# Hybrid attention and expert layer: the last expert's rows are added to the output on their own

## What is computed

```python
aff = jax.nn.softmax(jnp.einsum('bnd,de->bne', h, w_router).astype(jnp.float32), axis=-1)
gates, idx = lax.top_k(aff.swapaxes(1, 2), cap)            # cap = 128 tokens an expert
xe = h[bidx, idx]
hid = jax.nn.silu(jnp.einsum('becd,edf->becf', xe, w_gate)) * jnp.einsum('becd,edf->becf', xe, w_up)
ye = jnp.einsum('becf,efd->becd', hid, w_down) * gates[..., None].astype(h.dtype)
x = x + g2 * jnp.zeros_like(h).at[bidx, idx].add(ye)
return rms_norm(x, final_norm_g)
```

## Time and profile before

| | us |
|---|---|
| median of 3 runs | 2086.47 |
| lowest, highest | 2085.27, 2088.32 |
| the profiled execution's own time | 2086.9 |
| its span (first to last instruction) | 2085.1 |
| TensorE busy | 1858.8 (89%) |
| DVE busy | 1606.0 (77%) |
| ACT busy | 1303.9 (63%) |
| POOL busy | 270.8 (13%) |

### The profile page before, as it was taken

How to read it: one execution, slowest core, us unless ns; L and a number is a source line. 1 busy time by engine, 2 the same in 40 slices (tenths; PEclk the granted TensorE clock), 3 DMA queues, 4 the chain that set the end, 5 groups by cost and what they waited for, 6 DMA issues and landing times.

```text
span 2085.1 us, 28008 instructions
## 1 busy us (share of the span) xinstructions
PE 1858.8 (89%) x8691; PEld 1459.7 (70%) x8691; DVE 1606.0 (77%) x2065; ACT 1303.9 (63%) x1919; POOL 270.8 (13%) x291
## 2 busy tenths in 40 slices
PE   6799578998899899826999999999999999999993
PEld 3677456666666666515888888888888888888882
DVE  5577627668676766557999988889899989998983
ACT  3554127657566666524777777777777777777772
POOL 0233203101111110100111000110011001100011
PEclk8999779999999999957999999999999999999997
DMA  8356354101201110026999999999999999999985
GB/s 344 101 172 182 91 173 116 44 29 51 60 19 42 60 43 28 21 111 266 412 390 385 373 401 383 387 376 380 401 388 376 371 402 391 377 376 400 372 323 201
DMA packets 103794, 511.75 MB, mean 245 GB/s; under 512 B 12048, under 2 KB 36024, under 8 KB 53056
## 3 DMA queue, kind: packets, MB, share of 16 engines
q1 hardware_dynamic: 95824, 484.65, 61.4%
q0 software_dynamic: 4608, 16.78, 3.2%
q10 hardware_dynamic: 3312, 9.70, 1.3%
HBM read 481.19 MB, written 27.28 MB: 244 GB/s over the span
## 4 chain that ended last, share of the span: by engine, by line
PE 51%; issue 2%; DVE 2%; DMA 1%; ACT 0%; POOL 0%; ACTq 0%; POOLq 0%; SPq 0%
PE banks L1513 33%; PE banks L1538 16%; PE banks L1525 1%; PE banks L1494 1%; DVE topi L1384 1%; DVE top L1382 1%; DVE cand L1385 1%; DMA xe<-h_scratch,icol 0%; DMA acc_scratch<-ysc,idx_s 0%; DVE raw L1477 0%; ACT raw L1371 0%; DMA raw<-acc_scratch 0%; POOL fst L1298 0%; POOL fst L1300 0%; POOL gate_s L1281 0%
## 5 line engine op out<-in xcount | busy, mean ns | idle before, releaser
L1416 DVE TENSOR_TENSOR w_lo<-raw,w_hi 128x2048 fp32r<-128x2048 f32 x256 | 574.6, 2285 | 67.4 <-ACT w_hi L1320 67.4
L1320 ACT ACTIVATE w_hi<-raw 128x2048 fp32r<-128x2048 f32 x256 | 470.2, 1916 | 8.3 <-DMA raw<-in_w_exp 8.2
L1513 PE MATMUL banks<-w_hi,x_hi 128*128 128x512 f32 x1024 | 405.5, 396 | 1.4 <-DVE x_lo L1410 1.4
L1513 PE MATMUL banks<-w_hi,x_lo 128*128 128x512 f32 x1024 | 399.9, 390 | 0.0
L1513 PE MATMUL banks<-w_lo,x_hi 128*128 128x512 f32 x1024 | 399.4, 390 | 0.0
L1424 DVE TENSOR_TENSOR d_lo<-raw,d_hi 128x1024 fp32r<-128x1024 f32 x256 | 296.1, 1216 | 1.5 <-ACT d_hi L1342 1.4
L1342 ACT ACTIVATE d_hi<-raw 128x1024 fp32r<-128x1024 f32 x256 | 258.0, 1060 | 40.1 <-DMA raw<-in_w_exp 26.7
L1513 PEld LDWEIGHTS banks<-w_hi,x_lo 128*128 128x128 f32 x1024 | 192.7, 188 | 40.8
L1513 PEld LDWEIGHTS banks<-w_hi,x_hi 128*128 128x128 f32 x1024 | 192.9, 188 | 39.7 <-DVE x_lo L1410 1.8
L1513 PEld LDWEIGHTS banks<-w_lo,x_hi 128*128 128x128 f32 x1024 | 193.1, 189 | 38.1
L1014 DVE TENSOR_TENSOR ptl<-banks,pth 128x384 fp32r<-128x384 f32 x320 | 176.3, 554 | 56.0 <-ACT pth L960 51.7
(11 more groups left out here) (202 smaller groups left out, 2756.8 us busy)
## 6 DMA issues: line engine op xcount, KB each, us to landing
raw<-in_w_exp SPq DMA_DIRECT2D x384, 1024.0 KB, 7.8
a_ring<-in_w_mod SPq DMA_DIRECT2D x32, 512.0 KB, 4.7
qt<-q_scratch SPq DMA_DIRECT2D x64, 192.0 KB, 3.5
a_slot<-in_w_mod SPq DMA_DIRECT2D x8, 1024.0 KB, 12.3
a_w_raw<-in_w_in SPq DMA_DIRECT2D x3, 2048.0 KB, 30.8
q_scratch<-a_qst SPq DMA_DIRECT2D x16, 384.0 KB, 3.8
a_xt<-in_x ACTq DMA_DIRECT2D x8, 512.0 KB, 3.3
xr<-in_x SPq DMA_DIRECT2D x8, 512.0 KB, 4.1
```

The lines of the kernel that those rows point to most:

```text
L1320: act.activation(w_hi[which][c][:, :], raw[which][c][:, :], ACT.Copy).then_inc(s["hi_done"], 1)
L1416: dve.tensor_tensor(w_lo[which][c][:, :], raw[which][c][:, :], w_hi[which][c][:, :].bitcast(F32), ALU.subtract).then_inc(s["lo_done"], 1)
L1513: i = pe.matmul(psum[:, 2 * (j % 2) + which, :], x_[par][:, k, :], w_, start=(k == 0 and w_ is hi and x_ is x_hi), stop=(k == KD - 1 and x ...
```

## The change

The eight loads of `acc_scratch` no longer wait for the last expert: SP waits for 15 scatters and for the raw buffers, loads all eight tiles, and later issues the eight stores itself, each when its tile is normalised. POOL, once scatter 14 has landed, gathers the 128 rows of `acc_scratch` that expert 15 chose into `xe`. DVE normalises tiles 0 to 3, then makes the result of expert 15, adds `xe` to it (`ysc`), normalises tiles 4 to 7 and then `ysc` as a ninth set of rows. ACT's nine squares write their unused squares to two PSUM banks instead of a raw buffer, and `ysc` is the ninth. When the eight stores have landed, POOL writes `ysc` over the 128 rows of `out` with an indirect DMA (no addition), and the program's last wait is for that. Rows that expert 15 chose are so normalised twice, once without it, and the second version replaces the first.

The diff, without the hunks that only pass `out_rows` on:

```diff
@@ before.py +++ after.py @@
+    out_rows = out.rearrange("b n d -> (b n) d")
...
@@ -1187,18 +1188,18 @@
     h_hi, h_lo = (sb(f"h_{n}", [P, NK, P], F32R, M) for n in ("hi", "lo"))
     d_hi, d_lo = ([sb(f"d_{n}{k}", [P, D], F32R, M) for k in range(NK)] for n in ("hi", "lo"))
     ysc = sb("ysc", [P, D], F32, M)
+    sqj = psum[:, 0:2, :].rearrange("p a n -> p (a n)")
     carry = sb("carry", [P, 2], F32, M)
     fgain = sb("fgain", [P, D], F32, M)
 
     xa = [raw[t // 4][t // 2 % 2][:, t % 2 * D:(t % 2 + 1) * D] for t in range(TL)]
-    sqj = raw[2][0][:, 0:D]
-    fst = sb("fst", [P, TL, 3], F32, M)
+    LAST = TL
+    fst = sb("fst", [P, TL + 1, 3], F32, M)
     s = {n: sem("m_" + n) for n in (
         "top_order", "cand_zero", "cand_done", "merged", "carried", "top_done", "top_t", "cols_done", "idx_g", "x_in", "x_mm", "x_a", "x_b",
         "gate_mm", "up_mm", "sil_done", "hid_done", "ht_mm", "ht_done", "down_mm", "y_done", "y_out", "sel_done",
-        "hi_done", "lo_done", "d_hi_done", "d_lo_done", "h_lo_done", "fg_in", "a_done", "mean", "rstd", "norm_done")}
+        "hi_done", "lo_done", "d_hi_done", "d_lo_done", "h_lo_done", "fg_in", "a_done", "mean", "rstd", "norm_done", "last_sum", "last_out")}
     raw_in = [[sem(f"raw_in{w}{c}") for c in range(2)] for w in range(3)]
-    NX = TL
     xa_in = unit_in
     xa_out = sem("xa_out")
     Y, HB, XB = 4, 6, 7
@@ -1243,9 +1244,14 @@
             load(E - 1, NJ - 1, 2, 0)
             load(E - 1, NJ - 1, 2, 1)
 
-            sp.wait_ge(s["y_out"], 16 * E)
+            sp.wait_ge(s["y_out"], 16 * (E - 1))
             for t in range(TL):
+                if t % 2 == 0:
+                    sp.wait_ge(s["lo_done"], 4 * (NJ * E - 1) + t // 2 + 1)
                 sp.dma_start(xa[t][:, :], acc_d.rearrange("(t p) d -> t p d", p=P)[t]).then_inc(xa_in[t], 16)
+            for t in range(TL):
+                sp.wait_ge(s["norm_done"], t + 1)
+                sp.dma_start(out_d[t], xa[t][:, :]).then_inc(xa_out, 16)
 
         @block.gpsimd
         def _(pool):
@@ -1292,12 +1298,26 @@
                 gather(e + 2)
                 scatter(e)
             scatter(E - 2)
-            scatter(E - 1)
-            for t in range(TL):
+
+            pool.wait_ge(s["y_out"], 16 * (E - 1))
+            pool.tensor_copy(idx_s[:, :], icol[:, E - 1:E])
+            pool.tensor_copy(gate_s[:, :], gcol[:, E - 1:E]).then_inc(s["sel_done"], 1)
+            pool.wait_ge(s["sel_done"], E)
+            pool.wait_ge(s["x_mm"], 2 * E)
+            carrier(2 * E - 2)
+            pool.indirect_dma_start(out=xe[:, :], out_offset=None, in_=acc_d,
+                                    in_offset=bass.IndirectOffsetOnAxis(ap=idx_s[:, 0:1], axis=0)).then_inc(s["x_in"], 16)
+            for t in range(TL + 1):
                 pool.wait_ge(s["a_done"], t + 1)
                 pool.tensor_tensor(fst[:, t, 1:2], fst[:, t, 0:1], eps_c[:, 1:2], ALU.add).then_inc(s["mean"], 1)
                 pool.wait_ge(s["mean"], t + 1)
                 pool.tensor_tensor(fst[:, t, 2:3], fst[:, t, 1:2], eps_c[:, 0:1], ALU.pow).then_inc(s["rstd"], 1)
+            pool.wait_ge(xa_out, 16 * TL)
+            pool.wait_ge(s["norm_done"], TL + 1)
+            carrier(2 * E - 1)
+            pool.indirect_dma_start(out=out_rows, out_offset=bass.IndirectOffsetOnAxis(ap=idx_s[:, 0:1], axis=0),
+                                    in_=ysc[:, :], in_offset=None).then_inc(s["last_out"], 16)
+            pool.wait_ge(s["last_out"], 16)
 
         @block.scalar
         def _(act):
@@ -1362,17 +1382,13 @@
             split_down(E - 1, NJ - 1)
             turn(E - 1, NJ - 1)
 
-            def store(t):
-                act.wait_ge(s["norm_done"], t + 1)
-                act.dma_start(out_d[t], xa[t][:, :]).then_inc(xa_out, 16)
             for t in range(TL):
                 act.wait_ge(xa_in[t], 16 * 2)
                 after(act, s["a_done"], t)
-                act.activation(sqj[:, :], xa[t][:, :], ACT.Square, accum_out=fst[:, t, 0:1]).then_inc(s["a_done"], 1)
-                if t >= 1:
-                    store(t - 1)
-            store(TL - 1)
-            act.wait_ge(xa_out, 16 * NX)
+                act.activation(sqj, xa[t][:, :], ACT.Square, accum_out=fst[:, t, 0:1]).then_inc(s["a_done"], 1)
+            act.wait_ge(s["last_sum"], 1)
+            act.wait_ge(s["a_done"], TL)
+            act.activation(sqj, ysc[:, :], ACT.Square, accum_out=fst[:, LAST, 0:1]).then_inc(s["a_done"], 1)
 
         @block.vector
         def _(dve):
@@ -1467,15 +1483,27 @@
                     x_part(0, 0, 0)
                     x_part(0, 0, 1)
             every(expert, dve)
+            FIRST = 4
             dve.wait_ge(s["fg_in"], 16)
-            dve.tensor_scalar(fgain[:, :], fgain[:, :], ROOT, None, ALU.mult)
+            dve.tensor_scalar(fgain[:, :], fgain[:, :], ROOT, None, ALU.mult).then_inc(s["fg_in"], 16)
             split_down(E - 1, NJ - 1)
             turn(E - 1, NJ - 1)
+
+            def final(t, rows_):
+                dve.wait_ge(s["rstd"], t + 1)
+                if t == 0:
+                    dve.wait_ge(s["fg_in"], 32)
+                dve.scalar_tensor_tensor(out=rows_, in0=rows_, scalar=fst[:, t, 2:3], in1=fgain[:, :],
+                                         op0=ALU.mult, op1=ALU.mult).then_inc(s["norm_done"], 1)
+            for t in range(FIRST):
+                final(t, xa[t][:, :])
             result(E - 1)
-            for t in range(TL):
-                dve.wait_ge(s["rstd"], t + 1)
-                dve.scalar_tensor_tensor(out=xa[t][:, :], in0=xa[t][:, :], scalar=fst[:, t, 2:3], in1=fgain[:, :],
-                                         op0=ALU.mult, op1=ALU.mult).then_inc(s["norm_done"], 1)
+            dve.wait_ge(s["y_done"], E)
+            dve.wait_ge(s["x_in"], 16 * (E + 1))
+            dve.tensor_tensor(ysc[:, :], ysc[:, :], xe[:, :], ALU.add).then_inc(s["last_sum"], 1)
+            for t in range(FIRST, TL):
+                final(t, xa[t][:, :])
+            final(LAST, ysc[:, :])
 
         @block.tensor
         def _(pe):
```

More of the change, by code:

```diff
@@ L132, in build @@
         K.close()
-        nc_phase_m(nc, ctx, sem, sb, a, psum, ident, rows, aff, eps_c, h2_d, acc_d, out_d, unit_in)
+        nc_phase_m(nc, ctx, sem, sb, a, psum, ident, rows, aff, eps_c, h2_d, acc_d, out_d, out_rows, unit_in)
 def after(eng, sem_, v):
@@ L1151, in nc_phase_b, with nc_phase_m @@
     B.close()
-def nc_phase_m(nc, ctx, sem, sb, a, psum, ident, rows, aff, eps_c, h2_d, acc_d, out_d, unit_in):
+def nc_phase_m(nc, ctx, sem, sb, a, psum, ident, rows, aff, eps_c, h2_d, acc_d, out_d, out_rows, unit_in):
     G1, SH2, SC2, G2 = range(4)
```

## The result

The median of four runs is 2072.52 us (2069.51 to 2073.81), against 2086.94 for four runs of the kernel before. These two medians lie 14.4 apart. The ratio on record, which is not the quotient of the two medians, is 0.9923 with a 95% interval of 0.9909 to 0.9937, that is 13.1 to 19.0 us less. The profiled execution took 2071.5, its span 2069.6, 15.5 less than before; 14.1 of that lie in the tail and 1.4 ahead of it, as follows. The forecast was 12.2 less, 2074.7, in a range from 2071.5 to 2079.0.

What follows compares the result with a forecast made beforehand. The prediction took 32.8 us in series after TensorE's last matmul as the part to shorten. Early normalising, late result, stores and a final scatter gave span 2072.9, 12.2 less: 2086.9 - 12.2 = 2074.7 us, range 2071.5 to 2079.0.

Steps and rivals of the forecast that it cites:

- Multiplies 1, 2 and 3 keep the beat of 2.0, since each add is issued under the multiply ahead of it: DVE's normalising ahead of the last result: multiplies start 2.0 us apart, so the result starts at 2054.5 instead of 2052.27.
- Multiplies 4 to 7: DVE behind result and sum: 4 to 6 spaced 1.3 us, a 0.4 wait before 7, which ends at 2062.7.
- The last scatter: POOL's final indirect write to `out`: issued 2066.9, lands 5.5 us later at 2072.4; ends taken as 4.3 and 6.2.
- 0.5 follows to the end, as now: Program end: 0.5 us from the last scatter's landing at 2072.4 to the span's end at 2072.9.
- POOL in a gap doesn't hold DVE: Multiplies 4 to 7: POOL slips one operation into each gap between DVE's multiplies without delaying DVE.
- rival 2: POOL's powers for tiles 5 and 6 hold DVE, about 0.4 us each; total 2075.5; chance 0.12.
- Rival 1: The 2.0 us beat holds for every tile, DVE waiting for each power; multiply 7 ends 2064.3, total 2076.3; chance 0.22.
- rival 5: On SP's queue the early tile loads delay the last down weights; 2079.5, or 2090.7 at 200 GB/s; chance 0.04.
- Seven tenths of the normalising moves under TensorE: Tail of the kernel: this share of the normalising leaves the path, while a late scatter with its 6 us is added.
- Wrong if result starts before 2053: Sign on DVE's last result, forecast at 2054.5: an earlier start would mean the 2.0 us beat was not POOL's.
- The beat as what bounds the end before: Kernel before: eight normalisations run 2.0 us a tile, DVE busy 1.28 of it, because DVE waits for POOL's small operations.
- The range's low end: 2071.5: powers wholly off the path, result 2.1 us earlier and last 0.4 wait gone, giving 2072.2, plus some short-scatter chance.

Runs made afterwards that it cites:

- a_act_stores: Changed kernel with the stores back in ACT's queue behind each square, the ninth square behind all of them; ratio to before 0.9947 (0.9926 to 0.9967).
- a_mark: Changed kernel with one memset on POOL behind its last wait, as a mark; one run, 2072.8 us.
- a_noscat_sp: Changed kernel without the last scatter, with the wait for the eight stores on SP instead of POOL; one run, 2070.2 us.
- b_pool_waits: Kernel before with the wait for the eight stores on POOL instead of ACT; one run, 2084.1 us.
- a_early: Changed kernel with tile loads ahead of the last two down-weight loads, and more squares and multiplies under TensorE; ratio to before 0.9907 (0.9890 to 0.9924).
- b_sp_stores: Kernel before with the eight stores and the last wait on SP instead of ACT; ratio to before 1.0005 (0.9991 to 1.0018).
- a_no_scatter: Changed kernel without its last indirect DMA and the wait for it; ratio to before 0.9922 (0.9899 to 0.9945).
- a_best: Changed kernel with more work moved under TensorE and SP waiting for the last scatter; ratio to before 0.9906 (0.9889 to 0.9922), median 2066.98 us.

## Why the prediction was wrong in size

The direction and the order of events came out as written. The gain was put 1.9 too small in the tail, and the spread of the tail's start, which is chance, put 1.4 more on top. Several terms were wrong, and two of them cancelled. Every term, in + times:

| step | forecast | measured |
|---|---|---|
| first square | 0.65 | 0.47 |
| multiply 0 starts | 2.75 | 2.57 |
| result starts | 10.05 | 9.23 |
| multiply 7 ends | 18.25 | 16.55 |
| store 7 landed | 21.65 | 19.49 |
| last scatter issued | 22.45 | 19.92 |
| span ends | 28.45 | 26.52 |

- **"Multiplies 1, 2 and 3 keep the beat of 2.0, since each add is issued under the multiply ahead of it"** is the step that failed. In the kernel before, ACT's squares wait behind its stores, so each sum comes late:

```profile
2069.79 1.06 ACT L1371 ACTIVATE raw<-raw 128x1024 f32<-128x1024 f32 x1 [0.83 <-DVE raw L1477]
```

  The forecast itself had the sums 1.25 apart and never asked when POOL is free for the next one. Multiplies 1 to 3 came 1.73 apart, with the adds of tiles 2 and 3 ahead of the multiply and not under it. That is 0.54 of the 0.82 by which the result came early; a_act_stores gives exactly these 0.54 back. Of the rest, 0.18 is the first square, which began before the h_hi copy had ended.
- **Multiplies 4 to 7** at 1.3 and with a wait of 0.4: they took 1.22 each without one (0.73; another 0.15 came from result and sum ahead of them, 2.45 from start to start instead of 2.6). The row of four subtracts in 4.62 already had the overlap of neighbours; I used 1.28 and rounded up.
- **Store 7** landed after 2.9, not 3.3, and POOL's scatter was issued 0.43 behind it, not 0.8 (0.83 together).
- **The last scatter** landed after 3.4. The forecast's 5.5, from the gather, was 2.1 too long; the low bound from a plain store, 4.3, was too long as well. The fit of the Trainium skill, "DMA: Bandwidth & Descriptors", section "Anatomy of one DMA — SWDGE (gpsimd) path", gave 3.2 as an estimate, 0.2 below the measured 3.4.
- **"0.5 follows to the end, as now"** was 3.2, because the engine that ends last had changed from ACT to POOL (a_mark, a_noscat_sp, b_pool_waits). The errors of these two steps, 2.1 and 2.7, nearly cancelled, and the nearly right sum of 6.6 for 6.0 hid both.
- **POOL in a gap doesn't hold DVE**: right, four multiplies in 4.87 with POOL's operations between them; rival 2 is out. Rival 1 is out as well (no multiply from 4 to 7 waits). The Trainium skill, "SBUF — State Buffer", section "Who interferes with whom", has the one that issues first keep the shared ports for its whole instruction; here a power of 2053.82 ended at 2055.25 while DVE's multiply of 2054.76 ran on, so the measurement decides.
- **Early loads behind the weights** (rival 5): ACT's copies started at -4.99 and -2.27, as before. Not harmed; a_early shows that even the loads ahead of the last weights still fit. The gather, issued at 2012.0, landed after 10.5, some 30 ahead of the sum that needs it; its cost of nothing was not tested alone. The second down-weight load of the kernel before landed after 5.1 and not 4.9, which moved nothing.
- **"Seven tenths of the normalising moves under TensorE"** holds for the squares, six of eight; of the multiplies three of eight had ended when TensorE did.
- **"Wrong if result starts before 2053"**: it started at 2052.31, but with a tail that began 1.4 earlier. On the tail's clock the sign stood at +8.55, and +9.23 is behind it, so the sign does not speak against POOL's part in the beat.
- **The beat as what bounds the end before** was never priced against the transfers; b_sp_stores shows that they set the end there. The forecast didn't suffer, since it ended its chain with the stores of the changed kernel, of which the last took 2.9.
- The range's low end came from the powers off the path alone; it had no room for the wait of multiplies falling and the scatter being short at once, nor for 4 us either way in the start of the tail, which one profile couldn't show.

## What to carry to other kernels

An interval between repeated steps is a product of who is late in it: before it is carried over to a rearranged loop, ask for each wait in it whether its cause comes along. Moving work under another engine's time is worth what that engine leaves idle, so look for the next idle stretch (here ACT's 6 us before the last weight copies) and not only the one the change uses. Before a beat is taken for a stage's price, look at the DMA engines' share in the same window. And a new last instruction brings its own ending: name the engine that ends last and price what follows it.

## What the runs showed of the hardware

- The span ended 3.0 to 3.2 after POOL's last wait was met or its last instruction had ended (after, a_mark, a_no_scatter, b_pool_waits), 0.4 to 0.5 after when SP or ACT waited for plain stores (a_noscat_sp, before).
- A plain indirect write of 128 rows of 4 KB landed after 3.4 in all nine profiles that have it, against 6.2 to 6.3 for the quiet one that adds (before, b_pool_waits, b_sp_stores).
- A POOL one-column add issued 0.06 ahead of DVE's multiply ran in 0.18 beside it; issued under it, it ended 0.05 behind it.
- After a wait of 2.6 us (2.8 in a_best) TensorE's granted clock fell to 1.2 GHz in five of 14 profiles and stayed at 2.4 in nine; TensorE's end came 1.3 to 1.6 later for it.
- Eight loads and eight stores of 512 KB kept the DMA engines busy throughout, at 384 GB/s over 20 us (before, b_sp_stores).
